# Head norms' sums as two rounded products, unread column sums left out, and a planner with traced durations

## The reference, cut to what matters

```python
def rms_norm_2(x, g):
    xf = x.astype(jnp.float32)
    y = xf * lax.rsqrt(jnp.mean(xf * xf, axis=-1, keepdims=True) + NORM_EPS)
    return (y * g.astype(jnp.float32)).astype(x.dtype)
...
    q = apply_rope(rms_norm_2(q.reshape(B, S, DA_HEADS, 2, HEAD_DIM), q_norm), cos, sin)
    k = apply_rope(rms_norm_2(k.reshape(B, S, DA_HEADS, 2, HEAD_DIM), k_norm), cos, sin)
```

## Time and profile before

| | |
|---|---|
| runs, median of 3 | 1871.24 us (1871.17 to 1874.56) |
| profiled execution, own time | 1872.81 us |
| its span | 1870.7 us |
| PE busy | 1850.8 us, 99% |
| DVE busy | 1122.5 us, 60% |
| ACT busy | 785.5 us, 42% |
| POOL busy | 280.3 us, 15% |
| granted PE clock | 0.999 of full speed (2.4 GHz) |

### The profile page before, as it was taken

One profiled execution on the slowest core, in us unless ns is written; L12 is line 12 of the kernel. 1 busy time (PEld: TensorE's weight loads), 2 busy tenths in 40 slices (PEclk: granted clock), 3 DMA queues, 4 the chain that ended last, 5 costly groups with the idle time before them and its releaser, 6 DMA issues.

```text
span 1870.7 us, 24073 instructions
## 1 busy us (share of the span) xinstructions
PE 1850.8 (99%) x9098; PEld 1481.0 (79%) x9098; DVE 1122.5 (60%) x1974; ACT 785.5 (42%) x1728; POOL 280.3 (15%) x216
## 2 busy tenths in 40 slices
PE   9999999999999999999999999999999999999999
PEld 6887777888888888776678888888877788888887
DVE  7555896744454465588875535445978765445343
ACT  6435876322232232476643323223458533233221
POOL 2000551211010121111021101101210111011010
PEclk9999999999999999999999999999999999999999
DMA  6132000333333333322133323332342233323323
GB/s 232 58 103 67 24 1 24 94 98 102 91 101 94 98 90 102 102 79 74 52 98 94 100 93 101 92 101 85 102 118 64 63 95 97 102 91 101 95 91 96
DMA packets 51538, 166.56 MB, mean 89 GB/s; under 512 B 6880, under 2 KB 7264, under 8 KB 51168
## 3 DMA queue, kind: packets, MB, share of 16 engines
q1 hardware_dynamic: 51424, 165.03, 28.8%
HBM read 155.04 MB, written 2.10 MB: 84 GB/s over the span
## 4 chain that ended last, share of the span: by engine, by line
PE 89%; DVE 6%; ACT 1%; DMA 1%; issue 1%; SPq 1%; POOL 0%; DVEq 0%; ACTq 0%
PE bank L986 25%; PE bank L988 24%; PE bank L987 24%; PE bank L1095 2%; PE bank L1144 2%; DVE WL L1600 2%; PE bank L960 1%; PE bank L1222 1%; PE bank L962 1%; PE bank L961 1%; PE bank L1009 1%; PE bank L1174 1%; DVE GL L1609 1%; PE bank L1186 1%; PE bank L1119 1%
## 5 line engine op out<-in xcount | busy, mean ns | idle before, releaser
L1289 ACT ACTIVATE WH<-RAW 128x512 fp32r<-128x512 f32 (+2 forms) x584 | 332.1, 612 | 773.0 <-PE bank L988 682.0
L1600 DVE TENSOR_TENSOR WL<-RAW,WH 128x512 fp32r<-128x512 f32 (+2 forms) x584 | 464.4, 830 | 80.5 <-ACT WH L1289 74.8
L986 PE MATMUL bank<-GH,WH 128*128 128x512 f32 x1088 | 433.7, 399 | 0.7 <-DVE SM L1817 0.7
L986 PE MATMUL bank<-HH,WH 128*128 128x512 f32 x1056 | 423.2, 401 | 4.6 <-DVE TMP L1709 1.7
L988 PE MATMUL bank<-GH,WL 128*128 128x512 f32 x1088 | 424.0, 390 | 0.0
L987 PE MATMUL bank<-GL,WH 128*128 128x512 f32 x1088 | 423.6, 389 | 0.0
L988 PE MATMUL bank<-HH,WL 128*128 128x512 f32 x1056 | 411.7, 390 | 0.0
L987 PE MATMUL bank<-HL,WH 128*128 128x512 f32 x1056 | 411.3, 390 | 0.0
L2156 POOL TENSOR_TENSOR TMP<-TMP,RST 128x512 f32<-128x512 f32 x66 | 116.7, 1769 | 863.9 <-DVE TMP L2071 863.9
L986 PEld LDWEIGHTS bank<-GH,WH 128*128 128x128 f32 x1088 | 204.4, 188 | 48.7 <-issue 6.8
L986 PEld LDWEIGHTS bank<-HH,WH 128*128 128x128 f32 x1056 | 198.4, 188 | 54.7 <-issue 10.2
(11 more groups left out here) (246 smaller groups left out, 1864.6 us busy)
## 6 DMA issues: line engine op xcount, KB each, us to landing
RAW<-in_wgu SPq DMA_DIRECT2D x132, 512.0 KB, 3.5
RAW<-in_wd SPq DMA_DIRECT2D x48, 512.0 KB, 3.5
RAW<-in_wd SPq DMA_DIRECT2D x24, 384.0 KB, 3.1
RAW<-in_da_qk SPq DMA_DIRECT2D x16, 512.0 KB, 3.6
TMP<-TMP SPq DMA_DIRECT2D x104, 64.0 KB, 2.0
RAW<-in_w_inh SPq DMA_DIRECT2D x12, 512.0 KB, 3.6
RAW<-in_w_out SPq DMA_DIRECT2D x8, 512.0 KB, 3.7
RAW<-in_da_v SPq DMA_DIRECT2D x8, 512.0 KB, 3.5
```

The lines of the kernel that those rows point to most:

```text
L986: e.matmul(b, w_h, hi[st.x][k], start=(k == 0), stop=False)
L1289: e.activation(whs[s % NW][:, a:b], raw[s % NR][:, a:b], ACT.Copy).then_inc(S["wh"], 1)
L1600: e.tensor_tensor(wls[s % NR][:, a:b], raw[s % NR][:, a:b], whs[s % NW][:, a:b].bitcast(F), ALU.subtract).then_inc(S["wl"], 1)
```

## The change

1. The square of a head norm is made twice by ACT, once in float32 (SQB) and once rounded to float32r (`sq_hi`). POOL subtracts one from the other (`qsl`, tile `sq_lo`, both parts in SR, which lies over tiles that are free then). PE makes two rounded products with BR, the block ones as float32r, in place of the one in float32. POOL casts BR once (`consts`).
2. The column sums `lz4` and ACT's `lz5a` stay for j = 0, 2 and 4 alone. Their readers are the stages with tokens as rows (vg, hv, dv0, dv1, vs). The SiLU steps of the feed-forwards waited for them in the plan and now wait for the row factor `lz3a`.
3. The planner has a delay by waiting engine (`LAG`, `lag`), a price on PE for passages out of products that fill half the rows or columns (`turn`), and other durations for nearly every step; the diff shows those of the head norms and of `lazy`. An engine that finds nothing to do looks again at the next known time.

```diff
-    LAG = 200
+    LAG = {"PE": 330, "ACT": 145, "DVE": 130, "POOL": 150, "SP": 200}
...
+    def lag(self, a, b):
+
+        if a not in self.on:
+            return 0
+        return 210 if self.on[a] == "PE" and b == "ACT" else self.LAG[b]
+
+    @staticmethod
+    def turn(held, step):
+
+        if held not in ("rows", "cols"):
+            return 15 if held == "full" and step[0] == "tri" else 0
+        if step[0] == "tri":
+            return 210
+        return 0 if shape(step) in ("rows", "cols") else 150 if step[0] in ("tn", "nst", "dtp", "c_tp", "c_k2") else 195
...
-        o.add("ACT", ("qsq", *at), 500, of(st, m))
-        o.add("PE", ("qst", *at), 960, ("qsq", *at), st == "in" and ("lz4", 0), take=("nb", ("nr", *at)))
-        o.add("DVE", ("nr", *at), 620, ("qst", *at), ("lz2v", {"in": 0, "qk": 2, "ks": 4, "sq": 4}[st]),
+        o.add("ACT", ("qsq", *at), 1020, of(st, m))
+        o.add("POOL", ("qsl", *at), 1240, ("qsq", *at))
+        o.add("PE", ("qst", *at), 453, ("qsl", *at), st == "in" and ("lz4", 0), take=("nb", ("nr", *at)))
+        o.add("DVE", ("nr", *at), 602, ("qst", *at), ("lz2v", {"in": 0, "qk": 2, "ks": 4, "sq": 4}[st]),
               old or ("qn", st, m - 2) if not rope and m >= 4 else None)
-        o.add("ACT", ("rs", *at), 1200, ("nr", *at))
-        o.add("DVE", ("qn", *at), 680, ("rs", *at), st == "in" and ("xcv", 1), old)
+        o.add("ACT", ("rs", *at), 1187, ("nr", *at))
+        o.add("DVE", ("qn", *at), 662, ("rs", *at), st == "in" and ("xcv", 1), old)
...
-        o.add("PE", ("lz1", j), 1500, ("pag", 8 * j + 7), j == 0 and ("cf_in",), take=("nb", ("lz5a", j)))
-        o.add("DVE", ("lz2v", j), 700, ("lz1", j), kind="lz2v", first=-1, lands=800)
-        o.add("PE", ("lz4", j), 1000, ("lz2v", j), kind="lz4", first=-1)
-        o.add("ACT", ("lz3a", j), 1250, ("lz2v", j), first=-1)
-        o.add("ACT", ("lz5a", j), 450, ("lz4", j))
+        o.add("PE", ("lz1", j), 860, ("pag", 8 * j + 7), j == 0 and ("cf_in",), take=("nb", ("lz2v" if j % 2 else "lz5a", j)))
+        o.add("DVE", ("lz2v", j), 602, ("lz1", j), kind="lz2v", first=-1, lands=800)
+        o.add("ACT", ("lz3a", j), 1182, ("lz2v", j), first=-1)
+        if j % 2 == 0:
+            o.add("PE", ("lz4", j), 786, ("lz2v", j), kind="lz4", first=-1)
+            o.add("ACT", ("lz5a", j), 387, ("lz4", j))
...
+        pairs_only = ExitStack()
+        pairs_only.enter_context(nc.sbuf_tensor("PAD", [128, 12 * T], F))
+        SR = pairs_only.enter_context(nc.sbuf_tensor("SR", [128, 8 * T], R))
+        pairs_only.close()
+        BR = sbt("BR", 128, R)
+        sq_hi, sq_lo = [{st: SR[:, (c + k) * T:(c + k + 1) * T] for st, c in (("in", 0), ("qk", 6), ("ks", 2), ("sq", 2))}
+                        for k in range(2)]
...
             def lazy_column(j):
-                norm_bank("lz_ln", j + 1)
+                norm_bank("lz_ln", j // 2 + 1)
                 for i in range(4):
                     done = e.matmul(nb[:, 2 * i:2 * i + 2], ACC[:, i * 128:(i + 1) * 128], ones[:, 0:2],
                                     start=True, stop=True)
...
             def qst(st, m):
                 g = NM[st] + m
-                p.wait_ge(S["nm_sq"], g + 1)
+                p.wait_ge(S["nm_lo"], g + 1)
+                p.wait_ge(S["br"], 1)
                 norm_bank("nm_nr", g + 1)
-                e.matmul(nb, bones, sqb[1], start=True, stop=True).then_inc(S["nm_st"], 1)
+                e.matmul(nb, BR[:, :], sq_hi[st], start=True, stop=False)
+                e.matmul(nb, BR[:, :], sq_lo[st], start=False, stop=True).then_inc(S["nm_st"], 1)
...
             def lazy_column(j):
                 c = LBT[:, 24:28]
-                p.wait_ge(S["lz_pe"], j + 1)
+                p.wait_ge(S["lz_pe"], j // 2 + 1)
                 e.activation(c, nb[:, 0:8:2], ACT.Ln, bias=eps, scale=1.0 / 1024).then_inc(S["lz_ln"], 1)
-                p.wait_ge(S["lz_ln"], j + 1)
+                p.wait_ge(S["lz_ln"], j // 2 + 1)
                 e.activation(c, c, ACT.Exp, scale=-0.5).then_inc(S["lz_c"], 1)
...
                 p.wait_ge(S["unit"], unit_of(st, m))
                 if g:
                     p.wait_ge(S["nm_st"], g)
+                if st == "ks" and m == 0:
+                    p.wait_ge(S["vl"], SP_["s"])
+                    p.wait_ge(S["op"], OP["h4"] + 8)
                 b = ST[st].banks[m % len(ST[st].banks)]
                 e.activation(sqb[1], bank[b], ACT.Square).then_inc(S["nm_sq"], 1)
+                e.activation(sq_hi[st], bank[b], ACT.Square).then_inc(S["nm_sq"], 1)
...
-                b, r_ = token_rows("dv0" if j < 4 else "dv1", j % 4, 3)
+                b, r_ = token_rows("dv0" if j < 4 else "dv1", j % 4, 2)
...
             def e_vs(i):
-                b, r_ = token_rows("vs", i, 5)
+                b, r_ = token_rows("vs", i, 3)
...
-                p.wait_ge(S["lz_pe"], g // 8)
+                p.wait_ge(S["lz_a"], g // 8)
+                p.wait_ge(S["lz_pe"], (g // 8 + 1) // 2)
...
             def consts():
                 p.wait_ge(S["cii"], 16)
+                p.wait_ge(S["cf"], 16)
+                e.tensor_copy(BR[:, :], bones).then_inc(S["br"], 1)
                 e.tensor_copy(CI[:, :], p1(8, 1024)).then_inc(S["ci"], 1)
...
+            def qsl(st, m):
+                p.wait_ge(S["nm_sq"], 2 * (NM[st] + m + 1))
+                p.wait_ge(S["nm_st"], NM[st] + m)
+                e.tensor_tensor(sq_lo[st], sqb[1], sq_hi[st].bitcast(F), ALU.subtract).then_inc(S["nm_lo"], 1)
```

More of the change, by code:

```diff
@@ L93, in add @@
         q = self.queue[engine].setdefault(kind or step[0], [])
+        self.on[step] = engine
         q.append((step, ns, after, first, lands, take, self.n))
@@ L110, in longest @@
                 left[a] = left.get(a, 0) + 1
-        length = {i[0]: i[1] + i[4] + (self.LAG if e == "PE" else 60) for e, _, i in self.items()}
+        length = {i[0]: i[1] + i[4] + (200 if e == "PE" else 60) for e, _, i in self.items()}
         tail = {s: 0 for s in needs}
@@ L137, in ready @@
                 return None, giver
-            t = max(t, self.ends[a])
+            t = max(t, self.ends[a] + self.lag(a, engine))
         return t, giver
@@ L145, in forwards @@
         self.ends, self.taken, self.given, self.begin, order = dict(self.end), {}, [], {}, []
-        events, unit, idle = list(self.ends.values()), 0, 0
+        unit, idle, held = 0, 0, "tri"
         while len(order) < self.n:
             engine = min(free, key=lambda e: free[e])
-            now, best = free[engine], None
+            now, best, soon = free[engine], None, []
             for q in queue[engine].values():
@@ L152, in forwards @@
                     continue
-                t, giver = self.ready(q[0])
-                if t is None or t > now:
+                t, giver = self.ready(q[0], engine)
+                if t is None:
+                    continue
+                if t > now:
+                    soon.append(t)
                     continue
@@ L162, in forwards @@
             if best is None:
-                later = [t for t in free.values() if t > now]
-                events = [t for t in events if t > now]
                 idle += 1
@@ L169, in forwards @@
                     raise ValueError(f"no step can begin: {heads[:40]}")
-                free[engine] = min(later + events) if later or events else now + 1
+                free[engine] = min(soon + [now + 200])
                 continue
@@ L179, in forwards @@
                 unit = step[2]
+            if engine == "PE":
+                ns, held = ns + self.turn(held, step), shape(step)
             order.append(step)
@@ L182, in forwards @@
             free[engine] = now + ns
-            self.ends[step] = now + ns + lands + self.LAG
-            events.append(self.ends[step])
+            self.ends[step] = now + ns + lands
         return max(free.values()), order
@@ L220, in run, with shape @@
         return best[1]
+def shape(step):
+    if step[0] == "tri":
+        return "tri"
+    if step[0] in ("sc", "c_sc"):
+        return "rows"
+    return "cols" if step[0] == "vl" and step[1] != "d" else "full"
 def nsa(n):
@@ L259, in plan @@
         for c in range(2):
-            o.add("DVE", ("lo", s, c), 620, ("hi", s, c), kind="lo", first="split")
+            o.add("DVE", ("lo", s, c), 602, ("hi", s, c), kind="lo", first="split")
     def evacuated(name, m):
@@ L364, in head_norm @@
     def head_norm(a, h, after, old=None):
-        o.add("ACT", ("hsqa", a, h), 1000, after, old, ("hn", a, h - 1) if h else None)
-        o.add("PE", ("hst", a, h), 960, ("hsqa", a, h), take=("ar" if a == "h" else "nb", ("hrsa", a, h)))
-        o.add("ACT", ("hrsa", a, h), 1250, ("hst", a, h))
-        o.add("DVE", ("hn", a, h), 1400 if a == "h" else 680, ("hrsa", a, h), a == "h" and ("e_hv3", h + 8))
+        o.add("ACT", ("hsqa", a, h), 972, after, old, ("hn", a, h - 1) if h else None)
```

(19 more changed lines are left out.)

170 lines of the change are left out of this document (85 added, 85 removed).

## The result

| | us | against before |
|---|---|---|
| before, 4 runs | 1871.61 (1871.17 to 1874.56) | |
| the change, 4 runs | 1880.61 (1878.55 to 1882.27) | 1.0047 [1.0034, 1.0059] |

The forecast was 1853.3 in 1847 to 1862, faster. The change is slower, by 0.47%, some 9 us. The medians of those runs lie between 1871.6 and 1873.7 us, so a difference between kernels of two tables is good to about 2 us.

A forecast was written before the change was run, and what follows sets the result against it. PE, busy 1850.8 of 1870.7 us, was taken to bound the kernel. -13.0 products, -2.4 column sums, -0.4 passages, +2.4 chain, -4.5 planner = -17.9 from 1872.8: 1854.9, against the median 1853.3 us, range 1847 to 1862.

The forecast's parts named there:

- Products and records: Head norms on PE: 64 records of 0.39 us, a pair 0.453 us; 24 column-sum records gone; POOL about 325, ACT about 804.
- The column sums' sets: Three sets ahead of the feed-forwards (j = 1, 3, 5) go, at 0.79 us each: 2.4 us saved.
- Saved: 0.407 x 32 = 13.0 us: Head norms on PE: two rounded products (0.453 us) replace one full-precision product (0.86 us), 32 times.
- DVE is busy 60%: Holds of DVE by POOL's 32 subtractions, at most 31 us of DVE time, were counted as nothing on the path.
- the rule: Trainium skill page: a two-input SBUF VectorE instruction contends with a GpSimd instruction reading SBUF; the second blocks fully.
- the row of 0.97 us: At 1373.85 us a DVE pair of weight subtractions took 2.26 us against 1.29, held 0.97 us for POOL's product.
- the rival: DVE held by POOL decides: 24 heads in qk and sq lose 0.97 us each, +23 us, 1877, slower; chance 0.02.
- From then on 4 to 8 us of attention work: In qk after the first three waits, attention work was taken to cover the longer head-norm chain: no further wait.
- The first three waits: At qk's first units, PE waits on the longer norm chain: 1.25, 0.57 and about 0.5 us, +2.4 us together.
- I take a third, -4.5 us: The planner's new durations and delays recover a third of the 13.8 us of PE waits in the middle.
- My bounds: Planner term's range: 0 (new waits of the same size replace the old) to -12 us.
- I am wrong if idle PE grows past 20 us in the middle: Refutation sign: middle PE waits were expected near 12 us; above 20 or under 6 would count against the forecast.

The follow-up runs named there:

- f0: Kernel before, its order kept, with only the three unread sets of column sums taken out: 1868.95 us, 0.9977.
- f1: f0 with two ACT squares and two rounded products, both of the high part, per head norm, no subtraction: 1864.94 us, 0.9956.
- g1: f0 with one rounded square and one rounded product per head norm, low part left out, in before's order: 1859.56 us, 0.9935.
- q3: q1's planner, with one rounded square and one rounded product per head norm, low part left out: 1851.89 us, 0.9884.
- q1: The change with a flat 200 ns behind every planned step and no price for passages, new durations kept: 1870.77 us, 0.9987.
- q5: q1 with the head norm's subtraction on DVE in place of POOL: 1863.56 us, 0.9951.
- f3: Before's order, column sums out, the change's head norm at the old places, products awaiting POOL's subtraction: 1899.03 us, 1.0139.

## Why the prediction was wrong

**Products and records: right.** 0.45 us for the pair, the counts, POOL busy 325.9 (325 predicted), ACT 796.6 (804). The column sums' sets went at 0.95 us each where two of them stood (j = 1 and 5), 0.79 predicted, and the whole edit gave 4.0. The clock isn't the rest: at the same granted clock of 1.000, 0.999 and 0.998 f0 is still 3.6, 3.3 and 4.0 us under before. The traces show one more difference, in sq: before waits 1.74 us for DVE behind a late weight transfer, and f0 doesn't. Whether the missing sums do that or the transfer varies, no run shows.

**"Saved: 0.407 x 32 = 13.0 us, all on PE, so on the path wherever PE isn't waiting": the step that failed first.** With the second square as the only other change it gave 4.0 (f1). The page said 99% busy, and I took each saved microsecond for a saved one at the end. But PE arrives earlier at its next wait for DVE or ACT and waits longer there, in qk and sq for attention's chain, at the start and at ks for the second square. Without that square 9.4 to 12.1 of 20.3 us came through (g1, q3).

**"DVE is busy 60%, so my sum takes none of it on the path": wrong by about 4 us in the old order, by up to 7.2 in a planned one** (q1 to q5, with the shorter chain in it). I had the rule, the row of 0.97 us and the rival, and gave it 2 in 100, because the average busy share says that DVE has room. At the places where PE waits for DVE next it has none. The rival's price of 23 us was too high, its mechanism was right.

**"From then on 4 to 8 us of attention work stand in between, and I put the rest at nothing": wrong.** The first three waits were right in kind and smaller than forecast, 1.6 us together for 2.4. But the sum had no term for the six heads at the start, nor for later ones, and where the order wasn't made for it the awaited subtraction costs 20.1 us (f3). The change's order hides most of that; what the steps moved for it cost in turn, no run shows.

**"I take a third, -4.5 us" for the planner: wrong in sign.** It was +6.8 with the old work: -5.9 from durations with the new way of looking (near my term) and +12.8 from delays and passages, 5.5 of it by the traces beside the sparse attention, between h3 and f1. My bounds were 0 and -12. I had excluded a loss by "at worst new ones of the same size take their place", for which no row spoke. This is the largest single miss, 11 us.

The sum by the measured parts: columns -4.0, pair without subtraction -4.0, POOL's hold +4 to +7, planner +6.8; that is +3 to +6, where the change has +9.0. The rest is the awaited subtraction in a planned order, which no run measures by itself, and whatever does not add up between runs; this part stays open. "I am wrong if idle PE grows past 20 us in the middle" was the line that struck: idle PE is 38.1 in all, 4.2 of it ahead of the first trio at 8.73 us and 3.2 behind the last, so about 31 in the middle.

## What to carry to other kernels

On an engine that is 99% busy, don't count work taken out in full; price it by the next wait. Here a third came through with a second square added for it, and about half without. Look also at where a step's result is waited for: the same new work in the old order took 14.8 us less with its products up to two trios later. Before moving an elementwise step to an idle engine, look at what its neighbour does at that moment: here the "busy" DVE did the subtraction for less than POOL cost it. And a planner's model is a parameter to be measured: put in the durations alone first, then each delay by itself, since here durations read from the trace made a better order, and delays and passages a worse one. Compare runs at the same granted clock before giving a cause to the last few microseconds.

## What was not expected of the hardware

A two-input subtraction of 128x512 on POOL (1.28 to 1.80 us in the kernel after) stretches DVE's weight subtractions that run beside it: a pair took 1.97 us where 1.28 is free, and 2.75 beside a rotary product and a subtraction. The 32 of them cost DVE as much busy time as doing the 32 subtractions itself (1140.0 and 1140.6 us).

The granted clock of one and the same kernel differs from execution to execution, 1.000 to 0.996 in 19 of before, and the time with it, 1871.0 to 1876.9 us. The same waits of PE at 925 us stood ahead of a clock of 0.82 and 0.84 in one kernel's trace and of 1.00 in another's.
